# Two of six high-part buffers become homes of the weight ring in a two-layer decoder trunk

## The chip, the core and the metric

The kernel runs on one core of a Trainium2 chip, in one launch. The metric is device time in microseconds. TensorE (PE) does the matrix products, VectorE (DVE) and ScalarE (ACT) the elementwise work, GpSimd (POOL) some sums and the indirect transfers, and SyncE (SP) issues nearly all weight loads. PEld in the profile is TensorE's loading of the stationary operand, which overlaps its products.

## The reference

Two layers on 256 tokens of width 1024, in float32. Each has a mixer of three branches, a cross-attention to 256 memory tokens, and a feed-forward part: a dense SwiGLU in layer 0, and in layer 1 the top 2 of 8 experts:

```python
def moe_swiglu(h, w_router, w1, w3, w2):
    logits = (h @ w_router).astype(jnp.float32)
    top_val, top_idx = lax.top_k(logits, TOP_K)
    top_w = jax.nn.softmax(top_val, axis=-1)
    combine = jnp.sum(jax.nn.one_hot(top_idx, N_EXPERTS, dtype=jnp.float32) * top_w[..., None], axis=-2)
    out = jnp.zeros_like(h)
    for e in range(N_EXPERTS):
        out = out + combine[..., e:e + 1].astype(h.dtype) * swiglu(h, w1[e], w3[e], w2[e])
    return out
```

An expert has w1 and w3 of 1024 x 3584 and w2 of 3584 x 1024. All eight are read whole, 352 MB, most of what the kernel moves.

## The kernel before

**Chunks.** All weights lie in one stream of chunks of 128 x 2048 words (1 MB). Chunks 0 to 146 belong to the two mixers, the attention and the dense layer; from MOE = 147 on the experts take 8 x 42 = 336. Below, an expert chunk is counted from 0: chunk c is n = MOE + c. Two at a time they are one transfer of 2 MB (`fetch`), except those in home 3, which come as two of 1 MB (`fetch_loose`).

**Two parts.** A product in float32 is made of products of rounded operands. ACT copies a landed chunk, rounded, into a high-part buffer (`split` and `split_at`, L866), DVE subtracts that from the chunk and writes the remainder, the low part, over the chunk in its home (its own `split_at`, L1425), and TensorE multiplies with both. `hi_ready` and `lo_ready` count the two steps, and `w_used` counts the chunks that TensorE is done with. Eight expert chunks (`UNDIVIDED`) are not split at all: TensorE multiplies by them as they land (L2757).

**Homes and buffers.** An expert pair lives in one of six homes: 0 to 2 in the tensor raw, 3 (LOOSE) in memhat and half of h_hl, 4 and 5 (JOINING) in U. That is a ring of twelve chunks. SP walks the pairs in order: before it issues the load of pair q it waits until TensorE has used the pair that was in that home six pairs earlier (`sp.wait_ge(w_used, ...)`). Home 5 joins with the sixth pair, once the gathered rows have left U (`ga_done`, `hr_in`). There are six high-part buffers: three in whi, and three in wlo, which in the layers before held the low parts. So ACT may begin chunk c when chunk c - 6 has been used (`freed`).

**The work around it.** A step is 512 hidden columns of one expert: a gate product (two chunks), an up product (two) and a down product (two, of two steps before). Experts with up to 128 tokens (even places) and with up to 64 (odd places, `few`) alternate step by step, so that twelve chunks are one round of both. A chunk of the first kind costs TensorE twelve products of 512 columns (L2246 to L2248), of the second eight (L2762, L2763). ACT and DVE do their other work at fixed places between the splits: after split c = gate_end(s) + 3, ACT waits until the gate product of step s is made (`w_used`), reads it (L1276 for few, L1281 else) and then the transposed hidden rows (L1222, L1224), and only then splits chunk gate_end(s) + 4, which is four behind the chunk it waited for. `gate_end(s)` is the second gate chunk of step s. The last five steps are one few expert alone.

Of the kernel before, what the change touches and what calls it, by code (L numbers as in the profile page):

```python
# [4 lines left out]
F32 = mybir.dt.float32  # L5
# [25 lines left out]
RAW, SPLIT = 6, 3  # L31
# [33 lines left out]
MOE = BASE[1] + 57  # L65
# [5 lines left out]

RAW_CHUNKS, RAW_BANK = 6, (0, 2, 1, 3, 4, 5)
RING, LATER = 5, 1
LOOSE, JOINING = 3, 5
DEPTH = 2 * SPLIT
JOINED = 10
HALF = SLOTS // 2
FAR, CLEARED = 2048, 30
SUMMED = (0, 1, 2, 3, 4, 5)
# [13 lines left out]
TOTAL = NE * PER_E  # L93
# [113 lines left out]
def rotation():  # L207

    ring, last, at, before = [0, 1, 2, LOOSE, 4], {}, [], []
    for q in range(TOTAL // 2):  # L210
        if q == JOINED // 2:
            ring = [JOINING] + ring
        if q == TOTAL // 2 - RING:
            ring.remove(JOINING)
        i = ring.pop(0)
        ring.append(i)
        at.append(i)
        before.append(last.get(i))
        last[i] = q
    return at, before  # L220
# [4 lines left out]
             if not few_step(s) and ORDER[s][1] % 3 == 1 and (ORDER[s][0] or ORDER[s][1] in (1, 4,))]  # L225


def divided(n):

    return n + 1 - sum(i < n for i in UNDIVIDED)  # L230


LAST = MOE + TOTAL - 1
# [4 lines left out]
def trunk(nc, x_cols, mem_cols, columns, b_in, moe_router, final_g, stream, out):  # L238
    with ExitStack() as ctx:
# [6 lines left out]
        def aliased(name, dt):  # L246

            at, shape = homes[name]
            return nc.alloc_sbuf_tensor_at(f"{name}_alias", shape, dt, offset=at)

        def sem(name):
            return ctx.enter_context(nc.semaphore(name))


        raw = sb("raw", [P, RAW, CW])
        whi = sb("whi", [P, SPLIT, CW], F32R)
        wlo = sb("wlo", [P, SPLIT, CW], F32R)
# [128 lines left out]
        hrow = nc.dram_tensor("hrow", [S, D], F32).ap()  # L386
        ys = nc.dram_tensor("ys", [1 + (NE - 1) * SLOTS, D], F32).ap()

        raw_r, memhat_r, U_r = (aliased(name, F32R) for name in ("raw", "memhat", "U"))
        loose = (memhat[:].rearrange("p a b -> p (a b)"), h_plain[:, 4:DB, :, :].rearrange("p a t s -> p (a t s)"))  # L390
        loose_r = (memhat_r[:].rearrange("p a b -> p (a b)"), h_hl[:, 4:DB, :, :].rearrange("p a t s -> p (a t s)"))
# [5 lines left out]
        lo_ready = sem("lo_ready")  # L397
        w_used = sem("w_used")
        in_par, in_mem, in_small = (sem(s_) for s_ in ("in_par", "in_mem", "in_small"))
        in_x = [sem(f"in_x{i}") for i in range(4)]  # L400
        in_gain = sem("in_gain")
        in_part = [[sem(f"in_part{n}_{i}") for i in range(PIECES[n] - 1)] + [w_raw[n]] for n in range(PARTED)]
        part_hi, part_lo = sem("part_hi"), sem("part_lo")
# [72 lines left out]

            return (n - MOE) % RAW

        def home(n, of, of_U, of_loose):

            i, k = HOME_OF[(n - MOE) // 2], (n - MOE) % 2
            if i == LOOSE:
                return of_loose[k]
            if i in PAIRED:
                return of_U[:, PAIRED[i] + CW * k:PAIRED[i] + CW * k + CW]
            return of[:, 2 * i + k, :]

        def pair_home(i):

            if i in PAIRED:  # L490
                return U[:, PAIRED[i]:PAIRED[i] + 2 * CW]
            return raw[:, 2 * i:2 * i + 2, :].rearrange("p a w -> p (a w)")

        def pair_done(i):

            return w_pair[i] if i in PAIRED else w_raw[(MOE + 2 * i) % RAW]

        def landed(n):

            if n < MOE:  # L500
                return raw[:, spot(n), :], w_raw[n % RAW], 16 * (n // RAW + 1)
            q = (n - MOE) // 2
            i = HOME_OF[q]
            loads = HOME_OF[0:q + 1].count(i)
            if i == LOOSE:
                return home(n, raw, U, loose), w_loose[(n - MOE) % 2], 16 * loads
            if i not in PAIRED:
                loads += dense_loads((MOE + 2 * i) % RAW)
            return home(n, raw, U, loose), pair_done(i), 16 * loads

        def again(c):

# [2 lines left out]

        def hi_home(n):

            if MOE <= n < MOE + TOTAL and (n - MOE) % DEPTH >= SPLIT:
                return wlo[:, (n - MOE) % SPLIT, :]
            return whi[:, n % SPLIT, :]  # L520

        def lo_home(n):

            if MOE <= n < MOE + TOTAL:
                return home(n, raw_r, U_r, loose_r)
            return wlo[:, n % SPLIT, :]

        def freed(n):

            return n - (DEPTH if MOE + SPLIT <= n < MOE + TOTAL else SPLIT) + 1  # L530

        def x_at(q, pair):

# [84 lines left out]
        def _(sp):  # L618
# [59 lines left out]
            for q in range(TOTAL // 2):  # L678
                p, _ = chunk_of(2 * q)
                if p == len(which):  # L680
                    if p == 1:
                        sp.wait_ge(count_ready, 2)
                    which.append(sp.value_load(order[0:1, p:p + 1], min_val=0, max_val=NE - 1))
                if BEFORE[q] is not None:
                    sp.wait_ge(w_used, MOE + 2 * BEFORE[q] + 2)
                elif q < 3:
                    sp.wait_ge(lo_ready, MOE + 2 * q + 2 - RAW)
                elif q == LOOSE:
                    sp.wait_ge(w_used, MOE)
                    fetch_loose(q, 1, 0)  # L690
                    continue
                elif q == 4:
                    continue
                else:
                    sp.wait_ge(ga_done, 1)
                    sp.wait_ge(hr_in, 16)
                if HOME_OF[q] == LOOSE:
                    for k in range(2):
                        fetch_loose(q, k, which[p])
                else:  # L700
                    fetch(q, which[p])
# [2430 lines left out]
```

## Time and profile before

| | |
|---|---|
| device time, median of 3 runs | 1784.02 us (1783.2 to 1785.82) |
| the profiled execution, own time | 1785.54 us |
| its span | 1783.5 us |
| PE, PEld, DVE, ACT busy | 99%, 85%, 85%, 68% of the span |

The profile is of one execution. Its span is from the first to the last instruction of the program, and its own time is 2.04 us more. Busy shares are of the whole span; the experts take about its second half. A wait is named by the engine that waits, the line, and what released it.

### The profile page before, as it was taken

How to read it: one execution, taken by the hardware profiler on the slowest of the kernel's cores; microseconds unless marked ns; L12 is line 12 of the kernel's file. 1: busy time of each engine (PE TensorE's matmuls, PEld its weight loads, DVE VectorE, ACT ScalarE, POOL GpSimd, SP SyncE). 2: the span in 40 equal slices, each digit the busy share in tenths (PEclk: the TensorE clock that was granted, in tenths of full speed). 3: DMA queues.
4: the chain of work that ended last, by engine and by line, in shares of the span. 5: the costliest groups of instructions: out<-in, count | busy, mean ns of one | idle time of the engine just before them, and what ended most of it. 6: DMA issues, size and time to landing. Idle time of an engine off the chain costs nothing.

```text
span 1783.5 us, 24760 instructions
## 1 busy us (share of the span) xinstructions
PE 1757.4 (99%) x9998; PEld 1510.2 (85%) x9998; DVE 1521.5 (85%) x1444; ACT 1218.6 (68%) x1152; POOL 88.7 (5%) x92
## 2 busy tenths in 40 slices
PE   9999999999999999999999999999999999999997
PEld 9989899899999999899887887877878778787775
DVE  7999876576557999886579899999999999999996
ACT  5657754545445556655467788878878788888885
POOL 1000000010001000000020000001000010000210
PEclk9999999999999999999999999999999999999999
DMA  9454455345554544665459999999999999999994
GB/s 346 170 185 142 172 198 194 116 148 213 188 188 153 199 173 144 228 237 189 164 211 370 395 417 420 427 424 426 425 422 424 425 425 421 424 426 425 427 424 182
DMA packets 62836, 521.20 MB, mean 292 GB/s; under 512 B 7675, under 2 KB 15099, under 8 KB 19458
## 3 DMA queue, kind: packets, MB, share of 16 engines
q1 hardware_dynamic: 52304, 507.83, 71.7%
q0 software_dynamic: 2416, 6.83, 1.0%
q10 hardware_dynamic: 8002, 4.99, 0.9%
q8 instruction: 76, 1.25, 0.3%
q14 instruction: 38, 0.31, 0.0%
HBM read 512.79 MB, written 8.65 MB: 292 GB/s over the span
## 4 chain that ended last, share of the span: by engine, by line
PE 72%; DVE 17%; ACT 6%; issue 3%; DMA 2%; SPq 0%; ACTq 0%; DVEq 0%
PE psum L2260 15%; PE psum L2246 11%; PE psum L2248 11%; PE psum L2247 11%; PE psum L2261 8%; DVE raw_alias L1425 5%; PE psum L2762 4%; PE psum L2763 4%; DVE U_alias L1425 4%; ACT whi L866 3%; DVE wlo L1425 2%; DVE h_hl L1425 2%; PE psum L2757 1%; DMA U<-in_stream 1%; DVE memhat_alias L1425 1%
## 5 line engine op out<-in xcount | busy, mean ns | idle before, releaser
L866 ACT ACTIVATE whi<-raw 128x2048 fp32r<-128x2048 f32 (+1 forms) x228 | 428.8, 1893 | 64.7 <-PE psum L2261 50.0
L1425 DVE TENSOR_TENSOR wlo<-raw,whi 128x2048 fp32r<-128x2048 f32 (+1 forms) x144 | 326.3, 2267 | 132.5 <-ACT whi L866 132.2
L2260 PE MATMUL psum<-h_hl,whi 128*128 128x512 f32 x1216 | 431.3, 398 | 0.3 <-DVE U L1783 0.2
L2261 PE MATMUL psum<-h_hl,wlo 128*128 128x256 f32 x1216 | 340.9, 280 | 0.0
L2260 PEld LDWEIGHTS psum<-h_hl,whi 128*128 128x128 f32 x1216 | 228.2, 188 | 55.5 <-issue 1.1
L2261 PEld LDWEIGHTS psum<-h_hl,wlo 128*128 128x128 f32 x1216 | 229.7, 189 | 0.1
L2246 PE MATMUL psum<-act_hl,whi 128*128 128x256 f32 x720 | 206.1, 286 | 1.0 <-DVE wlo L1425 0.7
L2247 PE MATMUL psum<-act_hl,whi 128*128 128x256 f32 x720 | 203.7, 283 | 0.0
L2248 PE MATMUL psum<-act_hl,wlo 128*128 128x256 f32 x720 | 203.7, 283 | 0.0
L1425 DVE TENSOR_TENSOR raw_alias<-raw,whi 128x2048 fp32r<-128x2048 f32 x84 | 190.0, 2283 | 8.1 <-ACT whi L866 7.9
L1425 DVE TENSOR_TENSOR U_alias<-U,wlo 128x2048 fp32r<-128x2048 f32 x82 | 185.1, 2283 | 9.4 <-ACT wlo L866 9.3
L1425 DVE TENSOR_TENSOR raw_alias<-raw,wlo 128x2048 fp32r<-128x2048 f32 (+1 forms) x85 | 188.9, 2270 | 4.3 <-ACT wlo L866 4.2
L2763 PE MATMUL psum<-raw_alias,h_hl 128*128 128x512 f32 x416 | 162.4, 390 | 0.0
L866 ACT ACTIVATE wlo<-raw 128x2048 fp32r<-128x2048 f32 (+1 forms) x85 | 156.0, 1898 | 3.6 <-DMA raw<-in_stream 3.6
L2246 PE MATMUL psum<-whi,act_hl 128*128 128x512 f32 x384 | 152.8, 398 | 2.5 <-DVE U_alias L1425 1.3
L866 ACT ACTIVATE wlo<-U 128x2048 fp32r<-128x2048 f32 x82 | 151.5, 1907 | 2.2 <-PE psum L2248 1.6
L2248 PE MATMUL psum<-whi,act_hl 128*128 128x512 f32 x384 | 149.7, 390 | 0.0
L2247 PE MATMUL psum<-U_alias,act_hl 128*128 128x512 f32 x372 | 144.9, 390 | 0.0
L2246 PEld LDWEIGHTS psum<-act_hl,whi 128*128 128x128 f32 x720 | 138.0, 192 | 3.7 <-DVE wlo L1425 1.4
L2247 PEld LDWEIGHTS psum<-act_hl,whi 128*128 128x128 f32 x720 | 138.0, 192 | 0.2
L2248 PEld LDWEIGHTS psum<-act_hl,wlo 128*128 128x128 f32 x720 | 138.0, 192 | 0.0
L2762 PE MATMUL psum<-wlo,h_hl 128*128 128x512 f32 x336 | 134.4, 400 | 0.0
(359 smaller groups left out, 3285.8 us busy)
## 6 DMA issues: line engine op xcount, KB each, us to landing
raw<-in_stream SPq DMA_DIRECT2D x85, 2048.0 KB, 12.3
raw<-in_stream SPq DMA_DIRECT2D x141, 1024.0 KB, 4.8
U<-in_stream SPq DMA_DIRECT2D x55, 2048.0 KB, 12.2
memhat<-in_stream SPq DMA_DIRECT2D x28, 1024.0 KB, 11.7
h_hl_alias<-in_stream SPq DMA_DIRECT2D x28, 1024.0 KB, 13.7
ys<-ones ACTq DMA_DIRECT2D x7, 512.0 KB
raw<-in_stream SPq DMA_DIRECT2D x6, 512.0 KB, 3.9
xT<-in_x_cols ACTq DMA_DIRECT2D x4, 256.0 KB, 6.5
```

The lines of the kernel that those rows point to most:

```text
L866: act.activation(hi_home(n)[:, first:words], src[:, first:words], ACT.Copy).then_inc(hi_ready, 1)
L1425: dve.tensor_tensor(lo_home(n)[:, first:words], src[:, first:words], hi_home(n)[:, first:words].bitcast(F32), ALU.subtract).then_inc(lo_re ...
L2246: pe.matmul(o, st[0], mv[0], start=start, stop=False, **kw)
L2247: pe.matmul(o, st[0], mv[1], start=False, stop=False, **kw)
L2248: return pe.matmul(o, st[1], mv[0], start=False, stop=stop, **kw)
L2260: pe.matmul(o[:].rearrange("p (a b) -> p a b", a=2), st[0], mv, start=start, stop=False)
L2261: return pe.matmul(o[:, 0:256], st[1], mv[:, 0, :], start=False, stop=stop)
L2757: ins = pe.matmul(o, he_full[:, P * k:P * k + P], words[:, 512 * k:512 * k + 512], start=k == 0, stop=False)
L2762: pe.matmul(o, st, mv[0], start=start, stop=False)
L2763: return pe.matmul(o, st, mv[1], start=False, stop=stop)
```

## The change

Home 6 (LENT) is added, in the first two of the three slots of wlo. The ring is then seven homes, fourteen chunks: pair q waits for the pair seven before it. LENT joins with the sixth pair (as soon as `w_used` says that the last chunk but one before the experts has been used, for until then wlo holds dense low parts), and home 5 now joins with the seventh. What is left for high parts is whi and the last slot of wlo, four buffers; `high_slots` hands them out, the one used longest ago first, and ACT may begin chunk c when chunk c - 4 has been used (c - 5 for the four split chunks behind an undivided one). The loads of LENT are counted on the semaphore of the first input load, which is used once before. No product, copy or subtraction is added or removed.

```diff
--- before.py
+++ after.py
@@ -71,9 +71,9 @@
 
 RAW_CHUNKS, RAW_BANK = 6, (0, 2, 1, 3, 4, 5)
 RING, LATER = 5, 1
-LOOSE, JOINING = 3, 5
+LOOSE, JOINING, LENT = 3, 5, 6
 DEPTH = 2 * SPLIT
-JOINED = 10
+JOINED, LENT_AT = 12, 10
 HALF = SLOTS // 2
 FAR, CLEARED = 2048, 30
 SUMMED = (0, 1, 2, 3, 4, 5)
@@ -212,6 +212,8 @@
             ring = [JOINING] + ring
         if q == TOTAL // 2 - RING:
             ring.remove(JOINING)
+        if q == LENT_AT // 2:
+            ring = [LENT] + ring
         i = ring.pop(0)
         ring.append(i)
         at.append(i)
@@ -225,9 +227,29 @@
              if not few_step(s) and ORDER[s][1] % 3 == 1 and (ORDER[s][0] or ORDER[s][1] in (1, 4,))]
 
 
+def high_slots():
+
+    last = {i: i - SPLIT for i in range(SPLIT)}
+    last[2 * SPLIT - 1] = -1
+    slot, freed = [], []
+    for c in range(TOTAL):
+        if MOE + c in UNDIVIDED:
+            slot.append(None)
+            freed.append(None)
+            continue
+        i = c if c < SPLIT else min(last, key=lambda i: (last[i], i))
+        slot.append(i)
+        freed.append(last[i] + 1)
+        last[i] = c
+    return slot, freed
+
+
 def divided(n):
 
     return n + 1 - sum(i < n for i in UNDIVIDED)
+
+
+HIGH_SLOT, HIGH_FREED = high_slots()
 
 
 LAST = MOE + TOTAL - 1
@@ -386,6 +408,7 @@
         hrow = nc.dram_tensor("hrow", [S, D], F32).ap()
         ys = nc.dram_tensor("ys", [1 + (NE - 1) * SLOTS, D], F32).ap()
 
+        lent = aliased("wlo", F32)
         raw_r, memhat_r, U_r = (aliased(name, F32R) for name in ("raw", "memhat", "U"))
         loose = (memhat[:].rearrange("p a b -> p (a b)"), h_plain[:, 4:DB, :, :].rearrange("p a t s -> p (a t s)"))
         loose_r = (memhat_r[:].rearrange("p a b -> p (a b)"), h_hl[:, 4:DB, :, :].rearrange("p a t s -> p (a t s)"))
@@ -397,7 +420,8 @@
         lo_ready = sem("lo_ready")
         w_used = sem("w_used")
         in_par, in_mem, in_small = (sem(s_) for s_ in ("in_par", "in_mem", "in_small"))
-        in_x = [sem(f"in_x{i}") for i in range(4)]
+        in_x = [sem(f"in_x{i}" if i else "in_x0_w_lent") for i in range(4)]
+        w_lent = in_x[0]
         in_gain = sem("in_gain")
         in_part = [[sem(f"in_part{n}_{i}") for i in range(PIECES[n] - 1)] + [w_raw[n]] for n in range(PARTED)]
         part_hi, part_lo = sem("part_hi"), sem("part_lo")
@@ -476,23 +500,29 @@
 
             return (n - MOE) % RAW
 
-        def home(n, of, of_U, of_loose):
+        def home(n, of, of_U, of_loose, of_lent):
 
             i, k = HOME_OF[(n - MOE) // 2], (n - MOE) % 2
             if i == LOOSE:
                 return of_loose[k]
+            if i == LENT:
+                return of_lent[:, k, :]
             if i in PAIRED:
                 return of_U[:, PAIRED[i] + CW * k:PAIRED[i] + CW * k + CW]
             return of[:, 2 * i + k, :]
 
         def pair_home(i):
 
+            if i == LENT:
+                return lent[:, 0:2, :].rearrange("p a w -> p (a w)")
             if i in PAIRED:
                 return U[:, PAIRED[i]:PAIRED[i] + 2 * CW]
             return raw[:, 2 * i:2 * i + 2, :].rearrange("p a w -> p (a w)")
 
         def pair_done(i):
 
+            if i == LENT:
+                return w_lent
             return w_pair[i] if i in PAIRED else w_raw[(MOE + 2 * i) % RAW]
 
         def landed(n):
@@ -502,11 +532,13 @@
             q = (n - MOE) // 2
             i = HOME_OF[q]
             loads = HOME_OF[0:q + 1].count(i)
+            if i == LENT:
+                return home(n, raw, U, loose, lent), w_lent, 16 * (loads + 1)
             if i == LOOSE:
-                return home(n, raw, U, loose), w_loose[(n - MOE) % 2], 16 * loads
+                return home(n, raw, U, loose, lent), w_loose[(n - MOE) % 2], 16 * loads
             if i not in PAIRED:
                 loads += dense_loads((MOE + 2 * i) % RAW)
-            return home(n, raw, U, loose), pair_done(i), 16 * loads
+            return home(n, raw, U, loose, lent), pair_done(i), 16 * loads
 
         def again(c):
 
@@ -515,19 +547,22 @@
 
         def hi_home(n):
 
-            if MOE <= n < MOE + TOTAL and (n - MOE) % DEPTH >= SPLIT:
-                return wlo[:, (n - MOE) % SPLIT, :]
+            if MOE <= n < MOE + TOTAL:
+                i = HIGH_SLOT[n - MOE]
+                return (wlo if i >= SPLIT else whi)[:, i % SPLIT, :]
             return whi[:, n % SPLIT, :]
 
         def lo_home(n):
 
             if MOE <= n < MOE + TOTAL:
-                return home(n, raw_r, U_r, loose_r)
+                return home(n, raw_r, U_r, loose_r, wlo)
             return wlo[:, n % SPLIT, :]
 
         def freed(n):
 
-            return n - (DEPTH if MOE + SPLIT <= n < MOE + TOTAL else SPLIT) + 1
+            if MOE + SPLIT <= n < MOE + TOTAL:
+                return MOE + HIGH_FREED[n - MOE]
+            return n - SPLIT + 1
 
         def x_at(q, pair):
 
@@ -691,6 +726,8 @@
                     continue
                 elif q == 4:
                     continue
+                elif q == LENT_AT // 2:
+                    sp.wait_ge(w_used, MOE - 1)
                 else:
                     sp.wait_ge(ga_done, 1)
                     sp.wait_ge(hr_in, 16)
```

SP's queue where the experts begin, before: the loads of home 4, of 0 to 2, the second chunk of home 3 (h_hl), and home 5 (U) behind the waits for the gathered rows.

```order
L634 DMA U<-in_stream 128x4096 [waits xs_done]
L634 DMA raw<-in_stream 128x4096 [waits lo_ready] x3
L638 DMA h_hl_alias<-in_stream 128x2048 [waits w_used]
L634 DMA U<-in_stream 128x4096 [waits hr_in,ga_done]
L634 DMA raw<-in_stream 128x4096 [waits w_used] x3
L638 DMA memhat<-in_stream 128x2048 [waits w_used]
L638 DMA h_hl_alias<-in_stream 128x2048
```

And in the changed kernel, the same stretch: wlo_alias is the new home.

```order
L669 DMA U<-in_stream 128x4096 [waits xs_done]
L669 DMA raw<-in_stream 128x4096 [waits lo_ready] x3
L673 DMA h_hl_alias<-in_stream 128x2048 [waits w_used]
L669 DMA wlo_alias<-in_stream 128x4096 [waits w_used]
L669 DMA U<-in_stream 128x4096 [waits hr_in,ga_done]
L669 DMA raw<-in_stream 128x4096 [waits w_used] x3
L673 DMA memhat<-in_stream 128x2048 [waits w_used]
L673 DMA h_hl_alias<-in_stream 128x2048
```

A load of 2 MB (wlo) now stands ahead of the one that waits for `hr_in` and `ga_done`, and each later load stands one pair further on in the stream.

ACT in the round of chunks 73 to 80, before (whi and wlo on the left are high-part buffers, what stands on the right is the home; L1276 and L1224 read the gate product and the transposed rows):

```order
L866 ACTIVATE whi<-raw 128x2048 [waits w_used,w_raw3]
L866 ACTIVATE whi<-raw 128x2048 [waits w_used,w_raw5]
L866 ACTIVATE wlo<-raw 128x2048 [waits w_used,w_raw5]
L866 ACTIVATE wlo<-raw 128x2048 [waits w_used,w_raw1] x2
L866 ACTIVATE whi<-memhat 128x2048 [waits w_used,w_loose0]
L1276 ACTIVATE U<-psum 64x512 [waits w_used]
L1224 ACTIVATE act_hl<-psum 128x512 [waits e_tr]
L866 ACTIVATE whi<-h_hl_alias 128x2048 [waits w_used,w_loose1]
L866 ACTIVATE whi<-U 128x2048 [waits w_used,w_pair4]
```

The same round in the changed kernel (its L903, L1313 and L1261 are L866, L1276 and L1224 of before):

```order
L903 ACTIVATE whi<-raw 128x2048 [waits w_used,w_raw5]
L903 ACTIVATE wlo<-raw 128x2048 [waits w_used,w_raw1]
L903 ACTIVATE whi<-raw 128x2048 [waits w_used,w_raw1]
L903 ACTIVATE whi<-memhat 128x2048 [waits w_used,w_loose0]
L903 ACTIVATE whi<-h_hl_alias 128x2048 [waits w_used,w_loose1]
L903 ACTIVATE wlo<-U 128x2048 [waits w_used,w_pair4]
L1313 ACTIVATE U<-psum 64x512 [waits w_used]
L1261 ACTIVATE act_hl<-psum 128x512 [waits e_tr]
L903 ACTIVATE whi<-U 128x2048 [waits w_used,w_pair4]
L903 ACTIVATE whi<-wlo_alias 128x2048 [waits w_used,in_x0_w_lent]
```

The instructions stand in the same order, and each split waits for `w_used` before and after; the homes that are read have moved on by some pairs. The values waited for are `freed`'s, two chunks later than before.

## Rows read from the trace of the kernel before

**Rows 1.** The page, busy time of PE and data moved in forty slices.

```profile
PE 1757.4 (99%) x9998; PEld 1510.2 (85%) x9998; DVE 1521.5 (85%) x1444; ACT 1218.6 (68%) x1152; POOL 88.7 (5%) x92
...
GB/s 346 170 185 142 172 198 194 116 148 213 188 188 153 199 173 144 228 237 189 164 211 370 395 417 420 427 424 426 425 422 424 425 425 421 424 426 425 427 424 182
```

**Rows 2.** Waits by total, 1010 to 1750 us: total, times, longest.

```profile
ACT U L1276 <- PE psum L2763: 65.9, 22, 3.4
...
DVE U_alias L1425 <- ACT wlo L866: 8.9, 15, 1.1
...
PE psum L2762 <- DVE h_hl L1425: 6.6, 9, 1.3
...
ACT wlo L866 <- DMA raw<-in_stream: 2.5, 1, 2.5
```

**Rows 3.** Timeline of SP, one load: start, duration, what.

```profile
1104.86 0.33 SPq L634 DMA_DIRECT2D U<-in_stream  x1
```

**Rows 4.** DMA issues, 1104 to 1106 us; last number: issue to landing.

```profile
U<-in_stream SPq DMA_DIRECT2D x1, 2048.0 KB, 12.3
```

**Rows 5.** Timeline of SP where the experts begin.

```profile
909.63 0.33 SPq L638 DMA_DIRECT2D h_hl_alias<-in_stream  x1
922.49 0.33 SPq L634 DMA_DIRECT2D U<-in_stream  x1
```

**Rows 6.** Timeline of ACT, chunks 73 to 80.

```profile
1105.84 3.71 ACT L866 ACTIVATE whi<-raw 128x2048 fp32r<-128x2048 f32 x2
1109.44 5.52 ACT L866 ACTIVATE wlo<-raw 128x2048 fp32r<-128x2048 f32 x3
1114.86 1.92 ACT L866 ACTIVATE whi<-memhat 128x2048 fp32r<-128x2048 f32 x1
1120.17 0.60 ACT L1276 ACTIVATE U<-psum 64x512 f32<-64x512 f32 x1 [3.40 <-PE psum L2763]
...
1121.28 1.91 ACT L866 ACTIVATE whi<-h_hl_alias 128x2048 fp32r<-128x2048 f32 x1
1123.09 1.91 ACT L866 ACTIVATE whi<-U 128x2048 fp32r<-128x2048 f32 x1
```

**Rows 7.** Timeline of DVE, same chunks.

```profile
1107.78 4.49 DVE L1425 TENSOR_TENSOR raw_alias<-raw,whi 128x2048 fp32r<-128x2048 f32 x2 [0.83 <-ACT whi L866]
...
1112.80 6.68 DVE L1425 TENSOR_TENSOR raw_alias<-raw,wlo 128x2048 fp32r<-128x2048 f32 x3
1119.40 2.29 DVE L1425 TENSOR_TENSOR memhat_alias<-memhat,whi 128x2048 fp32r<-128x2048 f32 x1
...
1123.23 2.29 DVE L1425 TENSOR_TENSOR h_hl<-h_hl_alias,whi 128x2048 fp32r<-128x2048 f32 x1 [0.35 <-ACT whi L866]
1125.44 2.29 DVE L1425 TENSOR_TENSOR U_alias<-U,whi 128x2048 fp32r<-128x2048 f32 x1
```

**Rows 8.** Timeline of PE, ends of chunks 72 to 74, change from 79 to 80.

```profile
1113.39 0.39 PE L2248 MATMUL psum<-whi,act_hl 128*128 128x512 f32 x1
...
1116.11 0.39 PE L2248 MATMUL psum<-whi,act_hl 128*128 128x512 f32 x1
...
1117.93 0.39 PE L2763 MATMUL psum<-raw_alias,h_hl 128*128 128x512 f32 x1
...
1127.87 0.47 PE L2246 MATMUL psum<-whi,act_hl 128*128 128x512 f32 x1
```

**Rows 9.** Timeline of ACT near the end.

```profile
1753.68 1.92 ACT L866 ACTIVATE whi<-U 128x2048 fp32r<-128x2048 f32 x1 [1.45 <-DMA U<-in_stream]
```

**Rows 10.** Timeline of DVE near the end.

```profile
1755.63 2.29 DVE L1425 TENSOR_TENSOR U_alias<-U,whi 128x2048 fp32r<-128x2048 f32 x1 [1.51 <-ACT whi L866]
```

**Rows 11.** Timeline of PE near the end, chunk 332.

```profile
1757.97 0.80 PE L2762 MATMUL psum<-whi,act_hl 128*128 128x512 f32 x1 [2.29 <-DVE U_alias L1425]
...
1761.12 0.40 PE L2763 MATMUL psum<-U_alias,act_hl 128*128 128x512 f32 x1
```

**Rows 12.** Windows near the end; after the engines: PEclk, DMA share, GB/s.

```profile
1758.00:1760.00 2.00, 2.00 (x5) 1.63 (x6) 2.00 (x2) 1.46 (x1) 0.00 (x0) 0.50 0.10 37
```


## The prediction

> **What bounds the kernel now.** I read the page first, then the totals of waits over the experts' stage, then single timelines. The page says two things that can't both be the limit: TensorE is busy 99% of the span, and from the 23rd slice on the DMA engines move 417 to 427 GB/s, flat as a ceiling [rows 1]. The change gives transfers more room and takes room from ACT, so which of the two holds the stage decides its sign. Three readings settle it for me.
>
> First, the waits from 1010 to 1750 us [rows 2]. ACT, which is the first to touch a landed chunk, waits for a transfer once into wlo, 2.5 us, but 22 times, 65.9 us in all, for TensorE to finish the gate product that it has to read (L1276). DVE waits for ACT 15 times before a chunk of U, 8.9 us; TensorE waits for DVE nine times before a chunk of h_hl, 6.6 us. So the compute engines wait for each other in a ring, and hardly for data.
>
> Second, one load in mid-stage. It is issued at 1104.86 [rows 3] and lands 12.3 us later [rows 4], at 1117.2. That is chunk 80 and 81, home 4, and ACT reads chunk 80 at 1123.09 [rows 6]: it lay ready for 5.9 us. The issue itself had to wait for TensorE (w_used), and 2 MB at 425 GB/s are 4.9 us, so 12.3 us says that the transfer stood in a queue. The queue is full because consumers pace it, and data wait for ACT, not the reverse.
>
> Third, the end. There it is otherwise: ACT starts chunk 332 at 1753.68, after 1.45 us of waiting for its DMA [rows 9]; DVE idles 1.51 us for ACT [rows 10], TensorE 2.29 us for DVE [rows 11]. When the last expert runs alone, its chunks cost TensorE only eight products each, and the transfers have become the limit. That is the only place where the two extra chunks can pay.
>
> A page speaks against this reading. The Trainium skill ("Perfetto Trace Analysis", Identifying the Most-Contended Engine) says that matmul busy share is a bad measure of headroom, because matmuls overlap, and that weight-load share tells more; by it TensorE would have room and the transfers would be the bound. The trace agrees that the 99% prove little by themselves, but the 5.9 us of lying ready don't hang on it. What the page would make of the time is the first rival.
>
> **The change, part by part.** *Work.* No product, split, subtraction or byte is added: 0.
>
> *The head start.* SP issues h_hl at 909.63 and then stands until 922.49 for the gathered rows [rows 5]. In the changed kernel the 2 MB for LENT go out in that hole. From there every pair is issued one place earlier: transfers lead by two chunks, 4.9 us at 425 GB/s. If the transfer of LENT slows the rows' own write, home 5 waits longer, but it now holds chunks 12 and 13 instead of 10 and 11 and has 5 us more: 0.
>
> *Mid-stage, gain.* Chunks that already lie ready for 5.9 us lie ready for some 10: 0.
>
> *The end, gain.* Without the DMA wait DVE starts chunk 332 up to 1.5 us sooner [rows 10]; its idle there is no longer, so no more. Behind the hole of 2.29 us the granted clock is 0.50 from 1758 to 1760, the 1.2 GHz level [rows 12], and the eight products of chunk 332 start over 3.15 us (1757.97 to 1761.12, [rows 11]); at full clock eight such take 1.82 us from end to end, the distance of the ends of chunks 73 and 74 [rows 8], and their starts 1.6. If the hole shrinks to a few tenths the clock should hold: 1.5 us more. Together 3.0 us. Lower bound 0 (the tail is held by something else), upper bound 4.9, the whole lead.
>
> *Four buffers, the price.* Now ACT may begin chunk c only when TensorE has finished c - 4, not c - 6. Take the round of chunks 73 to 80. TensorE ends chunk 72 at 1113.39 + 0.39 = 1113.78, 73 at 1116.50, 74 at 1118.32 [rows 8], and 75 at 1120.14, since L1276 waited for it until 1120.17 [rows 6]; 70 and 71 are two and one lengths of 2.72 us before 72, 1108.3 and 1111.1. ACT started 74 at 1107.64 (the second of the pair from 1105.84), 75, 76 and 77 at 1109.44, 1111.25 and 1113.05 and 78 at 1114.86 [rows 6]. With four buffers these become 1108.4, 1111.1, 1113.9, 1116.6 and 1118.4, each 0 to 0.1 behind TensorE. A split takes 1.92 us. So:
> - ACT ends 78 at 1120.35, and L1276, queued behind it on ACT, starts 0.17 us late. Of its 3.40 us of idle nearly all has been eaten; what was free is free no more.
> - DVE subtracts 77 as the third of the run from 1112.80, at 1117.20 [rows 7]. It now can't before 1118.55, 1.35 us late. 78 follows at 1120.8 for 1119.40, two short operations too, and 79, which had 0.35 us of idle ahead, comes 1.1 us late, 80 as well.
> - TensorE begins chunk 80 at 1127.87 [rows 8]; its subtraction ended at 1125.44 + 2.29 = 1127.73 [rows 7]. There is no cover. TensorE is 1.1 us late, and everything that hangs on `w_used` with it.
>
> DVE gets some back at its next idle: 8.9 us over 22 rounds [rows 2] are 0.4 a round, so such a round costs 0.7 net. Where DVE was further behind ACT, the late split is covered for it, and only the 0.17 of L1276 reaches the chunk behind. There are 22 waits of L1276, so 22 rounds. If all were covered: 22 x 0.17 = 3.7 us. If all were like the worked one: 22 x 0.7 = 15 us. I take one in three as uncovered, because DVE must have run dry shortly before, as it had for 0.83 us ahead of chunk 73 [rows 7], which it does not in each round: 22 x (0.7 + 0.17 + 0.17) / 3 = 7.7 us. The delays add up, since TensorE has 6.6 us of such waits to give, part of which falls to rounds that are late on DVE too.
>
> *Sum.* 1783.5 + 7.7 - 3.0 = 1788.2 of span, 4.7 more. The profiled run's own time was 1785.54, 1.5 above the median of the three runs shown; against that median of 1784.02 the same difference gives **1788.7 us**.
>
> **Rivals.**
> - *The transfers are the bound.* The flat 425 GB/s speak for it, and the end of the stage is bound by them. Then two chunks of lead are worth 4.9 us wherever they are used, and ACT's late starts hide behind DVE's backlog: 1784.0 - 4.9 = 1779.1. Against it: the chunk that lay ready 5.9 us, and one wait of ACT in 740 us. It decides if the late splits cost under 1 us in all.
> - *It comes out even.* Only the 0.17 us of L1276 costs, 3.7 us, and the end gives back 3.0, because DVE shifts its idle into place: 1784.7. For it: the late split 77 has 1.35 us of lateness against DVE only, TensorE's own distance to the low part is long there. Against it: chunk 80 has none.
> - *The ring closes tighter.* Nearly each round costs what the worked one does, and the end returns nothing, as the last expert's splits wait as well: 1784.0 + 15 = 1799. ACT's idle of 3.40 us, eaten whole, speaks for it; against it that DVE runs back to back most of the time.
> - *The change does nothing.* ACT doesn't reach its limit and the lead isn't used: 1784. ACT is ahead by six chunks too seldom for this to be whole; it goes with the even case.
>
> **How the numbers follow.** The forecast's mechanism, uncovered rounds partly paid for by the end: 0.50, with its own range 1785 to 1792. Even or nothing: 0.23. Transfers are the bound: 0.17. Tight ring: 0.10. A measurement of this kernel tells about 0.2%, 3.6 us, from no change. Of the forecast's half, 0.40 lies more than that above 1784.0 and 0.10 within it; the even case is within it; of the transfer case 0.16 is faster. That makes 0.16 faster, 0.34 the same, 0.50 slower. The range that leaves out 2 in 10 reaches from half of the transfer case's gain, 1781, to 1794, ten over the median and two thirds of the tight ring's cost.
>
> **What would show it.** In the changed profile: a load of 2 MB issued near 910 us; ACT's splits of whi and wlo, which now wait for a transfer once, waiting for TensorE in every round, some 1 to 3 us each time, and L1276's 65.9 us of waiting mostly gone into these; DVE's waits for ACT longer by 5 to 10 us in sum; TensorE's waits for DVE up by about as much; from issue to landing over 14 us in mid-stage instead of 12.3; no wait of ACT for a DMA near the end, TensorE without the hole before chunk 332 and clock 1.00 there. The prediction is wrong if DVE's waits for ACT don't grow (then covered rounds are the rule), if ACT still waits for transfers at the end (the lead was not kept), or if the rounds of twelve chunks get shorter than before, which would say that transfers paced them.

## The result and the profile after

The changed kernel takes 1792.05 us (median of 6 runs, 1791.48 to 1792.44), the kernel before 1784.28 us beside it (6 runs, 1782.97 to 1786.32). The ratio is 1.0044, 95% interval 1.0033 to 1.0054: slower by 7.8 us. The profiled execution took 1792.12 us, at the median of its kernel, with a span of 1790.0, 6.5 more than before. The profiled execution of the kernel before took 1785.54 us, 1.3 above its median of 1784.28. That is why the traces lie 6.5 us apart and the medians 7.8.

The page of the changed kernel, busy times and data moved, as in [rows 1]:

```profile
PE 1758.8 (98%) x9998; PEld 1508.3 (84%) x9998; DVE 1523.8 (85%) x1444; ACT 1230.8 (69%) x1152; POOL 83.3 (5%) x92
...
GB/s 344 176 179 141 182 195 188 118 148 209 185 186 172 190 165 142 247 235 188 142 288 377 392 419 415 426 424 412 417 415 425 418 422 410 425 423 421 420 428 139
```

PE, DVE and ACT have as many instructions as before. TensorE's busy time is up by 1.4 us and the span by 6.5, so 5.1 us are idle time of TensorE. ACT's busy time is up by 12.2 us for the same 1152 instructions: two splits back to back overlap a little (3.71 us for two, where one alone takes 1.92, [rows 6]), and fewer of them now stand back to back. From the 24th slice on the row of GB/s has lost its flatness: 410 to 428 where before had 417 to 427. The transfers now move less than their ceiling at times, and that already speaks against them as the bound.

The waits of the changed kernel, 1010 to 1750 us (total, times, longest), to lay beside [rows 2]:

```profile
ACT whi L903 <- PE psum L2285: 53.3, 69, 1.1
ACT U L1318 <- PE psum L2285: 22.0, 19, 2.2
ACT wlo L903 <- PE psum L2285: 15.5, 21, 0.8
...
DVE raw_alias L1462 <- ACT whi L903: 7.5, 15, 0.8
PE psum L2799 <- DVE raw_alias L1462: 6.9, 10, 1.3
...
PE psum L2799 <- DVE wlo L1462: 2.6, 3, 0.9
```

ACT's line L903 is the split (L866 of before). In these two rows it waits for TensorE 90 times, 68.8 us. The 65.9 us that ACT waited at L1276 are gone from the list altogether (the line is L1313 now). ACT hasn't more idle time, it has it elsewhere: added up over all rows of this view, its waits for TensorE make 106.6 us before and 105.0 after, but in 67 pieces before and 141 after. What is new is behind ACT. All waits of DVE for a split sum to 18.2 us (31 of them) before and 24.2 us (47) after; those of TensorE for DVE to 8.4 us (19) and 15.2 us (37).

The round that the prediction worked through, on ACT:

```profile
1108.82 1.92 ACT L903 ACTIVATE wlo<-raw 128x2048 fp32r<-128x2048 f32 x1 [0.69 <-PE psum L2285]
1111.82 1.92 ACT L903 ACTIVATE whi<-raw 128x2048 fp32r<-128x2048 f32 x1 [1.08 <-PE psum L2285]
1114.26 1.92 ACT L903 ACTIVATE whi<-memhat 128x2048 fp32r<-128x2048 f32 x1 [0.52 <-PE psum L2285]
1116.98 1.92 ACT L903 ACTIVATE whi<-h_hl_alias 128x2048 fp32r<-128x2048 f32 x1 [0.80 <-PE psum L2285]
1118.80 1.91 ACT L903 ACTIVATE wlo<-U 128x2048 fp32r<-128x2048 f32 x1
1120.73 0.59 ACT L1313 ACTIVATE U<-psum 64x512 f32<-64x512 f32 x1
```

These are chunks 74 to 78 and the read of the gate product. What was one idle piece of 3.40 us ahead of that read [rows 6] is now four short ones ahead of the splits, and the read itself has none.

The same round on DVE, chunks 77 and 78, and on TensorE, the start of chunks 79 and 80:

```profile
1118.93 2.29 DVE L1462 TENSOR_TENSOR h_hl<-h_hl_alias,whi 128x2048 fp32r<-128x2048 f32 x1 [0.43 <-ACT whi L903]
1121.14 2.29 DVE L1462 TENSOR_TENSOR U_alias<-U,wlo 128x2048 fp32r<-128x2048 f32 x1
```

```profile
1126.87 0.50 PE L2799 MATMUL psum<-whi,act_hl 128*128 128x512 f32 x1 [0.43 <-DVE U_alias L1462]
...
1129.16 0.47 PE L2283 MATMUL psum<-whi,act_hl 128*128 128x512 f32 x1 [0.18 <-DVE wlo L1462]
```

A late split has become a wait of DVE, and that a wait of TensorE, within three chunks.

The end of the stage: the load for chunks 332 and 333 on SP and its time from issue to landing (last number), ACT's reading of them, and TensorE's start of 332, to lay beside [rows 9, 11]:

```profile
1735.77 0.33 SPq L669 DMA_DIRECT2D wlo_alias<-in_stream  x1
```

```profile
wlo_alias<-in_stream SPq DMA_DIRECT2D x1, 2048.0 KB, 16.8
```

```profile
1761.32 3.71 ACT L903 ACTIVATE whi<-wlo_alias 128x2048 fp32r<-128x2048 f32 x2
```

```profile
1765.81 0.50 PE L2799 MATMUL psum<-whi,act_hl 128*128 128x512 f32 x1 [0.69 <-DVE wlo L1462]
```

The pair landed at 1735.77 + 16.8 = 1752.6, 8.8 us before ACT read it. TensorE's hole is 0.69 us instead of 2.29, and its first product takes 0.50 us instead of 0.80.

**Where the time goes, chunk by chunk.** The trace has the time of each increment of `w_used`, the end of each chunk on TensorE. This is how much later than in the kernel before a chunk ends, in us, worked out from the two traces:

| chunk | 10 | 43 | 67 | 79 | 127 | 163 | 211 | 247 | 295 | 331 | 332 | 335 |
|---|---|---|---|---|---|---|---|---|---|---|---|---|
| after | -0.6 | 0.1 | 0.4 | 1.1 | 3.0 | 4.1 | 6.0 | 7.2 | 9.0 | 9.4 | 6.4 | 6.4 |

From -0.56 to 9.44: the price of four buffers is 10.0 us. The 0.56 are there before the first expert chunk, so the change has no part in them; the traces of the other versions below lie 0.2 to 1.1 us ahead there.

The price comes in steps, most of them at the chunks 43, 55, 67, 79 and so on, and at the one behind. Counted from chunk 34, so that no step is cut in two, 24 stretches of twelve chunks reach to 322. Ten of them lose 0.59 to 0.91 us (8.0 in all), nine 0.15 to 0.21 (1.6 in all), one 0.40, and four nothing (-0.07 to 0.06). But for the two ends of the stage the pattern repeats every 84 chunks, two experts. Then chunk 332 gives back 3.04 us at once.

Which rounds are costly can be read from the trace before the change. There DVE waited for ACT 1.08 to 1.66 us in each of the ten costly rounds, about 1.1 in three of the nine cheap ones, and at most 0.28 in each of the other eleven. From 1200 to 1700 us it was busy 486.9 of 500 us, so there is little time in which a late split could be made good.

### The profile page after: what moved, and what is told of

It is laid out like the page before. It is cut to its first block, busy times and chain, and to the rows that moved or that the text cites. A ratio compares the mean times of both kernels' runs of the same rounds, so it can differ in the third digit from the quotient of the medians.

```text
span 1790.0 us, 24746 instructions
## 1 busy us (share of the span) xinstructions
PE 1758.8 (98%) x9998; PEld 1508.3 (84%) x9998; DVE 1523.8 (85%) x1444; ACT 1230.8 (69%) x1152; POOL 83.3 (5%) x92
## 4 chain that ended last, share of the span: by engine, by line
PE 71%; DVE 20%; ACT 6%; issue 2%; DMA 1%; SPq 0%; ACTq 0%; DVEq 0%
PE psum L2297 15%; PE psum L2283 13%; PE psum L2285 13%; PE psum L2284 12%; PE psum L2298 8%; DVE raw_alias L1462 6%; DVE U_alias L1462 4%; DVE wlo L1462 4%; ACT whi L903 4%; PE psum L2794 1%; PE psum L2818 1%; PE psum L2799 1%; PE psum L2800 1%; ACT wlo L903 1%; DVE h_hl L1462 1%
## 5 line engine op out<-in xcount | busy, mean ns | idle before, releaser
L903 ACT ACTIVATE whi<-raw 128x2048 fp32r<-128x2048 f32 (+1 forms) x252 | 475.5, 1896 | 88.6 <-PE psum L2298 50.0
L1462 DVE TENSOR_TENSOR raw_alias<-raw,whi 128x2048 fp32r<-128x2048 f32 x108 | 244.7, 2284 | 11.6 <-ACT whi L903 11.1
L2283 PE MATMUL psum<-whi,act_hl 128*128 128x512 f32 x552 | 222.6, 403 | 3.6 <-DVE raw_alias L1462 2.8
L2285 PE MATMUL psum<-whi,act_hl 128*128 128x512 f32 x552 | 215.4, 390 | 0.0
L1462 DVE TENSOR_TENSOR U_alias<-U,whi 128x2048 fp32r<-128x2048 f32 x68 | 154.6, 2284 | 6.0 <-ACT whi L903 5.8
L903 ACT ACTIVATE whi<-U 128x2048 fp32r<-128x2048 f32 x68 | 129.9, 1915 | 19.9 <-PE psum L2285 19.8
L2799 PE MATMUL psum<-whi,h_hl 128*128 128x512 f32 x336 | 133.8, 398 | 0.0
L2283 PEld LDWEIGHTS psum<-whi,act_hl 128*128 128x128 f32 x552 | 103.7, 188 | 32.2 <-issue 11.3
L2285 PEld LDWEIGHTS psum<-whi,act_hl 128*128 128x128 f32 x552 | 103.6, 188 | 22.5
L2284 PE MATMUL psum<-raw_alias,act_hl 128*128 128x512 f32 x300 | 116.8, 389 | 0.0
L1570 DVE SCALAR_TENSOR_TENSOR U<-U,par 128x256 f32<-128x256 f32 x240 | 99.2, 481 | 0.1
## 6 DMA issues: line engine op xcount, KB each, us to landing
wlo_alias<-in_stream SPq DMA_DIRECT2D x24, 2048.0 KB, 11.3
```

The lines of the kernel that those rows point to most:

```text
L903: act.activation(hi_home(n)[:, first:words], src[:, first:words], ACT.Copy).then_inc(hi_ready, 1)
L1462: dve.tensor_tensor(lo_home(n)[:, first:words], src[:, first:words], hi_home(n)[:, first:words].bitcast(F32), ALU.subtract).then_inc(lo_re ...
L1570: ins = dve.scalar_tensor_tensor(aacc[:, c, :], src, w, aacc[:, c, :], op0=ALU.mult, op1=ALU.add)
L2283: pe.matmul(o, st[0], mv[0], start=start, stop=False, **kw)
L2284: pe.matmul(o, st[0], mv[1], start=False, stop=False, **kw)
L2285: return pe.matmul(o, st[1], mv[0], start=False, stop=stop, **kw)
```

## The experiments

All times are medians; each ratio is to the kernel before, run beside it. Rows and chunk times are of the profiled execution.

**The buffers alone.** The changed kernel with the head start taken away: LENT never joins, and home 5 joins with the sixth pair as before.

```diff
-JOINED, LENT_AT = 12, 10
+JOINED, LENT_AT = 10, -2
```

> The changed kernel's four high-part buffers alone: home 6 is taken out again, so the ring is six homes, twelve chunks, as before. Theory: the whole price is that ACT waits for TensorE's use of chunk c - 4. TensorE should end chunk 331 some 9 to 10 us later than before, as in the changed kernel, and the two homes are worth nothing on top, since once the rounds are 10 us slower in sum the transfers catch up by themselves: 1791 to 1792 us, and no wait for a DMA ahead of chunk 332. Rival A: the two homes are what gave back 3.0 us at chunk 332; then this is 3 us slower than the changed kernel, 1795. Rival B: the loads into the new home, not the buffers, slow the rounds; then this is like before, 1784.

Measured: 1791.74 us, ratio 1.0043 (1.003 to 1.0057). Chunk 331 ends 9.4 us late and 332 6.3 us, as in the changed kernel. So the two added homes are worth nothing there, not even at the end: the 3 us are given back without them. A stage that runs 10 us longer lets the transfers catch up by itself. It also rules out that the loads into the new home slow the rounds, since there are none here.

**Five buffers.** The same, with a fifth high-part buffer handed out.

```diff
-    last[2 * SPLIT - 1] = -1
+    last[2 * SPLIT - 1], last[2 * SPLIT - 2] = -1, -2
```

> Five high-part buffers, twelve homes: ACT waits for chunk c - 5. Theory: in the round of chunk 78 ACT would start it at 1116.6 instead of 1114.86, still 2 us ahead of DVE's turn, so nothing is late: 1784 us, within 1.5. Rival: any buffer taken away costs its share; half of the price of two buffers, 1789.

Measured: 1783.88 us, ratio 0.9998 (0.9989 to 1.0007). Chunks lie 0.6 to 0.8 us ahead of the kernel before up to 324, with no steps. Two of its waits, 1010 to 1770 us:

```profile
ACT U L1313 <- PE psum L2800: 36.5, 22, 1.7
...
ACT whi L903 <- PE psum L2285: 15.4, 21, 0.8
```

Giving up the sixth buffer makes splits wait for TensorE, too, and eats ACT's idle ahead of the gate product, 65.9 to 36.5 us. It costs nothing, for some is left at every one of the 22 places. It ends in a hole like that of before, by its TensorE timeline and its window (behind the engines stand the granted clock, the DMA share and GB/s):

```profile
1757.58 0.50 PE L2799 MATMUL psum<-wlo,act_hl 128*128 128x512 f32 x1 [2.34 <-DVE U_alias L1462]
```

```profile
1758.00:1760.00 2.00, 2.00 (x13) 1.70 (x12) 2.00 (x2) 1.86 (x1) 0.00 (x0) 1.00 0.04 14
```

In the kernel before a hole of 2.29 us is followed by a clock of 0.50, the 1.2 GHz level [rows 11, 12]; here one of 2.34 us is followed by 1.00, the 2.4 GHz level. The eight products of chunk 332 start within 1.72 us of each other (1757.58 to 1759.30), in the kernel before within 3.15, and the chunk alone gains 1.4 us (from 0.44 us ahead to 1.84). That prices the half clock at 1.4 us, with the idle left as it was. The medians, 1783.88 and 1784.1 us, don't show it. So other executions of either kernel may have gone another way there; only one of each has a trace.

**Three buffers**, the other side, with twelve homes.

```diff
-    last[2 * SPLIT - 1] = -1
```

> Three high-part buffers, twelve homes: ACT waits for chunk c - 3. Theory: TensorE's use of c - 3, then 1.9 us of ACT and 2.3 us of DVE, 4.2 us, against the 3.6 to 4.6 us that TensorE takes for the two chunks left: the loop itself binds, in every round and at most chunks. Each pair of few chunks (3.6 us) misses by 0.6 us or more plus what stands between on ACT and DVE, some six chunks in a round of 28 rounds: 60 to 200 us slower, 1850 to 1980. Rival (the price grows evenly, 4 us a buffer): 1796.

Measured: 1848.25 us, ratio 1.0366 (1.0351 to 1.038). Two of its waits, 1010 to 1790 us:

```profile
ACT whi L902 <- PE psum L2284: 138.0, 132, 4.1
DVE raw_alias L1461 <- ACT whi L902: 60.6, 87, 2.3
```

That is just below the expected 1850 to 1980. Chunk 331 ends 65.7 us late, by steps of 1.4 to 3.1 us in each round, and 332 gives back 3.05 once more. The price of six, five, four and three buffers is 0, 0, 10 and 66 us on TensorE. That is a knee: as long as ACT's idle absorbs the later starts they cost nothing; behind it some rounds pay (four) and then all of them (three).

**One transfer more, in both kernels.** If transfers were the bound, 2 MB more would cost 4.9 us in either kernel, and if they are covered, nothing. A copy of 2 MB from the stream to an unused place in device memory goes ahead of pair 60 (chunk 120), in the kernel before and in the changed one.

```diff
+        spare = nc.dram_tensor("spare", [P, 2 * CW], F32).ap()
...
+                if q == 60:
+                    sp.dma_start(spare, pair_of(0)).then_inc(in_par, 16)
...
+            sp.wait_ge(in_par, 32)
```

> The kernel before with one useless transfer of 2 MB from one place in device memory to another, issued on the same queue ahead of pair 60, in mid-stage. Theory: landed chunks lie ready for 6 us there, so nothing is felt at once, but the last loads come later by what the transfer takes of the engines, and the end hangs on them: 4 to 8 us slower, all of it from chunk 320 on. Rival (rounds hold the time to the end, the wait for a DMA ahead of chunk 332 is covered otherwise): no difference, 1784.

> The changed kernel with the same useless transfer. Theory: its chunks lie ready for about 9 us at the end, so the transfer is not felt at all: 1792 us, within 1.5, with chunk 332 not waiting. Rival (the transfers pace the stage, which is why it shows 410 to 428 GB/s): 4 to 8 us slower, 1796 to 1800.

Measured: before with the copy 1790.43 us, ratio 1.0035 (1.0021 to 1.0049); after with the copy 1791.63 us, ratio 1.004 (1.0027 to 1.0054), nothing on top. In the kernel before the copy doesn't delay TensorE for 80 chunks (chunk 199 is 0.6 us ahead). ACT feels it at once. Without the copy it waits for a transfer five times (7.1 us), always behind 1728 us; with it 56 times, from 1220 us on. Two of its rows, 1010 to 1770 us:

```profile
ACT whi L870 <- DMA raw<-in_stream: 22.9, 26, 2.2
ACT wlo L870 <- DMA raw<-in_stream: 18.7, 16, 3.1
```

The median time of a load of 2 MB into raw, from issue to landing, is 17.4 us from 1100 to 1740 us, where it was 12.9: what the copy took is still owed for the rest of the stage. Chunk 319 is 1.5 us late, so it isn't all from chunk 320 on, as expected; 324 is 3.7 late, 332 5.0, where 2 MB at 425 GB/s are 4.9. Against the 0.5 us that it was ahead it is 5.5, and the copy also has its 2 MB to write. So the kernel before is bound in two ways that lie close to each other. In mid-stage the engines set the pace, with data ready (no wait of ACT for a transfer from 1010 to 1728 us). But the transfers run at their ceiling all the while and save up hardly anything, and what they lose anywhere they owe at the end. The changed kernel is slow enough that a whole load fits in.

**Five buffers and thirteen homes.** This is what the runs so far point to: the fifth buffer is needed, the sixth isn't, so one slot of wlo can be lent. It needs homes of one chunk, and here every load is one of 1 MB. Its control has the same small loads with twelve homes.

```diff
-                sp.dma_start(pair_home(i), pair_of(chunk_of(2 * q)[1], e)).then_inc(pair_done(i), 16)
...
+                sp.dma_start(place(i, raw, U, loose, lent), pair_of(chunk_of(c - k)[1], e)[:, CW * k:CW * k + CW])\
+                  .then_inc(done_at(i)[0], 16)
```

> Five high-part buffers and thirteen homes of one chunk each; every expert chunk is a transfer of its own of 1 MB. Theory: five buffers cost nothing, and a lead of one chunk, 2.5 us, covers the 1.45 us that ACT waited for its DMA ahead of chunk 332: the 3.0 us of the end come without the price, 1781 us, faster than both kernels. Rival: each buffer less costs its share, or smaller transfers move less per us: 1784 or more.

> The control of the thirteen homes: five buffers, twelve homes of one chunk, transfers of 1 MB. Theory: a chunk is asked for as soon as its own home is free instead of its pair's, which leads by less than a chunk and only where the queue runs empty: 1783 to 1784 us. Rival: the lead of a chunk is already had by this, then as the thirteen homes, 1781.

Measured: thirteen homes 1786.27 us, ratio 1.0011 (1.0002 to 1.002); the control 1789.13 us, ratio 1.0027 (1.0017 to 1.0038). Neither came out as expected (1781 and 1783 to 1784 us). The thirteenth home is worth 2.9 us between the two, but the small loads cost 5.3 us (the control against five buffers with loads of 2 MB). The page of the former says where:

```profile
GB/s 346 177 178 142 180 198 189 119 144 210 188 188 158 201 171 142 231 235 187 178 225 397 391 417 419 422 420 421 420 421 420 421 421 421 421 420 421 421 421 188
...
q1 hardware_dynamic: 72464, 507.84, 72.3%
```

421 GB/s in mid-stage instead of 425, with 72464 packets for the same bytes instead of 52304. One per cent of rate over 740 us is 7 us of transfer by estimate, which is owed at the end: the control's TensorE is in step with the kernel before up to chunk 310, and 6.3 us late at 331.

**The same with loads of 2 MB.** The homes are laid side by side in the order of the ring, so that a load of a pair fits any two neighbours; two of thirteen pairs straddle a gap and go as two loads. The ring keeps all homes to the last chunk, and the last norm's gains lie elsewhere.

```diff
         raw = sb("raw", [P, RAW, CW])
+        wlo = sb("wlo", [P, SPLIT, CW], F32R)
         whi = sb("whi", [P, SPLIT, CW], F32R)
-        wlo = sb("wlo", [P, SPLIT, CW], F32R)
-        h_hl = sb("h_hl", [P, DB, 2, S], F32R)
         act_hl = sb("act_hl", [P, 4096], F32R)
         xT = sb("xT", [P, DB, S])
+        h_hl = sb("h_hl", [P, DB, 2, S], F32R)
         memhat = sb("memhat", [P, DB, S])
...
+        joined = c % 2 == 0 and HOME_OF[c] != WLO_HOME and HOME_OF[c + 1] == HOME_OF[c] + 1
+        chunks[c] = 2 if joined else 1
...
-        gfin = u(2048, D)
+        gfin = u(6144, D)
```

> Five buffers for high parts and a ring of thirteen homes, with the transfers of 2 MB kept: the homes now lie side by side in SBUF in ring order, so that a pair of chunks goes in one transfer into any two neighbours (two of thirteen pairs are still two transfers of 1 MB), the ring keeps all its homes to the last chunk, and the gains of the last norm lie in another place. Theory (the buffers below five cost the time, lead counts only at the end, and the size of transfers cost what five_thirteen lost): every chunk up to 324 within 1 us of the kernel before, ACT's wait for the transfers ahead of chunk 332 shrunk by a chunk's lead to under 1 us, TensorE ending 2.5 to 4 us earlier than before; time 1780 to 1782, ratio 0.998. Rival (the transfers are what bounds the whole expert stage, so that lead piled up anywhere is worth time): gains are spread along the stage, the end 5 us or more early. Rival (any home added costs its ring's price, as in four high-part buffers): 1786 or later, with lateness growing by round.

Measured: 1782.26 us (11 runs, 1781.18 to 1783.04), ratio 0.9992 (0.9983 to 1.0002). Chunks lie 0.95 to 1.1 us ahead of the kernel before from the first to 331, a lead that is there before the experts begin. Chunk 332 is 4.05 us ahead: 3.0 at the end and nothing in between. That the ring keeps all its homes moves, of the loads of the kernel before, only that of the last pair, behind chunk 332, and there nothing more is gained (335 is 4.06 us ahead). ACT's and TensorE's start of the chunk that stood in the hole, 332, and the page's data rate:

```profile
1750.84 1.91 ACT L883 ACTIVATE wlo<-run_b 128x2048 fp32r<-128x2048 f32 x1
```

```profile
1755.34 0.50 PE L2779 MATMUL psum<-wlo,act_hl 128*128 128x512 f32 x1 [0.66 <-DVE run_br L1442]
```

```profile
GB/s 346 174 182 142 177 196 194 115 149 213 188 185 155 194 175 143 227 243 189 166 232 357 396 418 426 427 425 424 425 418 425 425 427 425 425 424 426 426 426 185
```

The profiled span is 1779.3 us, 4.2 less than before, the medians differ by 1.95. The profiled execution, 1781.18 us, is the fastest of the eleven, and that of the kernel before lies 1.3 us above its median, so the two traces show more than the medians do. The interval just includes 1, so this version isn't shown to beat the kernel before. Against the changed kernel it is 9.8 us faster, and that is far outside both intervals.

## Why the prediction was right or wrong

**The forecast held.** Predicted were 1788.7 us in a range of 1781 to 1794, measured 1792.05; slower, inside the range. The likeliest case, uncovered rounds partly paid for at the end, is the one that happened. But 4.7 us more were forecast and 7.8 came. Of these 3.1 us, 1.8 lie between the spans (6.5 against 4.7): the price came out 2.3 larger, and 0.56 were won by luck, for the traced execution was that much ahead when the experts began, which no term had. The other 1.3 come from carrying the difference of the spans over to the median, though the profiled execution of the kernel before lay above it.

**What bounds the kernel: right, but not whole.** That mid-stage is a ring of engines that wait for each other, and not of transfers, is shown by the buffers: with twelve homes and four of them the whole loss is there. That the end was "the only place where the two extra chunks can pay" is borne out for one chunk by the version with thirteen homes, ahead by a constant 1 us until 331 and by 4 from 332. The prediction counted one wait of ACT for a transfer in 740 us; there are three from 1010 to 1750 us, 4.5 us in all, but all behind 1728 us, so the reading stands. What the reading missed is how near the transfers are. 5.9 us of lying ready looked like cover; it is cover for a chunk, but the copy of 2 MB shows that lost transfer time isn't made good in more than 200 chunks. A backlog says what waits now, not at which rate it is used up. The rule of the Trainium skill ("Perfetto Trace Analysis", Identifying the Most-Contended Engine), to judge TensorE's headroom by weight-load share and not by matmul busy time, was weighed as the first rival. For the place that this change touched the trace decides against it, for transfers owe nothing until the end; for the kernel's next gain it points the right way, as the copy in the kernel before shows.

**The worked round: right, nearly to the tenth.** At chunk 72 the changed kernel was 0.38 us late. With that added, the splits were predicted at 1108.8, 1111.5, 1114.3, 1117.0 and 1118.8; they started at 1108.82, 1111.82, 1114.26, 1116.98 and 1118.80, one of them 0.3 off. The gate read was predicted at 1120.34 + 0.38 and came at 1120.73; DVE's subtraction of 77 at 1118.55 + 0.38, it came at 1118.93. TensorE reaches chunk 80 at 1129.16 instead of 1127.87, and less the 0.38 that is 0.91 us; predicted were 1.1, of which DVE was to get 0.4 back. It got nothing back: the whole round, chunks 70 to 82, loses 0.91. The place was off by one: most of it, 0.73, is lost at the start of chunk 79.

**The price of four buffers: mechanism right, size off.** The sum gave 7.7 us (7.6, if it is worked out), measured are 10.0. The two prices of a round were nearly right: 0.17 for a covered one, where nine rounds lost 0.15 to 0.21, and 0.7 for an uncovered one, where ten lost 0.59 to 0.91, 0.80 on average. The term that failed is "I take one in three as uncovered": it was chosen and not read, and ten of 24 were. Covered rounds came to 2.5 us in the sum, and all but the ten lost 2.0; uncovered ones came to 5.1, and lost 8.0. The condition that the prediction named for the costly kind, that DVE had run dry shortly before, could have been looked up in the trace of before: it holds in all ten, and misleads in only three cheap rounds, where DVE had also waited 1.1 us. One round had been worked out, where the pattern spans two experts.

**The end: right size, wrong reason.** 3.0 us were predicted and 3.04 came, between the two traces. Its two halves hold there: five buffers keep the hole and lose only the half clock, 1.4 us, which leaves 1.6 for the idle (predicted 1.5 and 1.5). Between the medians less may have come: the profiled execution of the kernel before lies 1.3 us above its median, about what the half clock cost it. That this is the reason is not shown. But the gain was put down to the head start of two chunks. Without it the same 3.0 us come back (the buffers alone, 3.05), and with three buffers too. A stage that is 10 us longer gives the transfers 10 us, and one chunk's lead is enough. In the changed kernel the head start wasn't what paid. With five buffers, where rounds are as fast as before, one chunk of it did. So the two added homes bought what the slowness gave for nothing.

**The head start itself: right.** The load of LENT goes out in SP's hole, and mid-stage gains nothing. By SP's timeline, beside [rows 5]:

```profile
909.05 0.33 SPq L673 DMA_DIRECT2D h_hl_alias<-in_stream  x1
909.42 0.43 SPq L669 DMA_DIRECT2D wlo_alias<-in_stream  x1
922.75 0.33 SPq L669 DMA_DIRECT2D U<-in_stream  x1
```

**The signs.** DVE's waits for ACT were to grow by 5 to 10 us, they grew by 6.0, TensorE's for DVE by as much, they grew by 6.8; ACT's splits wait for TensorE in all rounds, three or four times in nearly each, though 0.8 us on average and at most 1.1, not 1 to 3; no wait for a DMA near the end, no large hole, clock 1.00 there. One sign was wrong: from issue to landing "over 14 us in mid-stage instead of 12.3". It fell. The medians from 1100 to 1740 us are 12.9 us before and 10.9 (raw) and 11.3 (U) after. I had thought that loads issued earlier stand longer in the queue. But a load is still issued when TensorE frees its home, and TensorE became slower: the queue ran shorter, as the dips in the row of GB/s show. That it is 11.2 and 10.9 with the buffers alone says that the homes have no part in it.

**The rivals.** The transfers as the bound (1779.1): refuted for mid-stage by the buffers alone and by the copy that costs the changed kernel nothing. Even (1784.7): refuted, for ten rounds of 24 cost 0.59 us or more. The tighter ring (1799): uncovered rounds are more than a third, but far from nearly each, and the end does return something. A ring in which every round pays is what three buffers make.

## What to carry to other kernels

Where one pool of memory is shared between two depths (landed data, worked buffers), price each by taking it away alone: here giving up the sixth high-part buffer was free, giving up the fifth cost 10 us and the fourth 56 more, while the landed side gained at most 3 us and only at the end. Take from a depth until the idle time that covers it is nearly eaten, and no further, and look for that in the wait that grows shorter (65.9, 36.5, none) before any wait behind it grows. A total that repeats by rounds should be read over a whole period of the pattern, not from one round and a guessed share; where one engine's earlier wait is the condition (here DVE's for ACT), that wait can be counted round by round before anything is built. And a difference between two traces is one between medians only where each profiled execution lies at the median of its kernel.

## What the runs showed of the hardware

The granted clock after an idle hole isn't a matter of the hole's length alone: 2.29 us were followed by 0.50 in the kernel before, 3.00 us by 0.64 from 1762 to 1764 in the kernel before with the copy, and 2.34 us by 1.00 with five buffers, with the same products behind it. Between those with 2.29 and 2.34 us it was worth 1.4 us. These are three kernels with one trace each, and what decided between them no run here settles. Two versions compared by their traces can differ by as much from this alone.

Loads of 1 MB into 128 partitions moved 421 GB/s where loads of 2 MB moved 425, with several in flight all the time (a load of 1 MB into raw landed 14.8 us after its issue, by the median of the control); in a kernel with its transfers at the ceiling that was 5.3 us. The Trainium skill ("DMA: Bandwidth & Descriptors", Measured (HBM→SBUF, 128 partitions, SWDGE, issued from GpSimd)) gives 341 GB/s for a transfer of 1 MB and 425 for 16 MB, and a rule to batch to 1 MB or more. Those were issued from another engine than the loads here; for this kernel the measurement decides: loads of 1 MB moved 421 GB/s and not 341, and going on from 1 MB to 2 MB still pays, by one per cent of the rate.
